# Modulation weight of an adaLN decoder block: products on TensorE in four column tiles in place of VectorE sums, x loaded first

## What is computed

```python
ada = silu(c) @ w_ada + b_ada            # (1024) @ (1024, 6144): one row of 6144
shift1, scale1, gate1, shift2, scale2, gate2 = split(ada, 6)
u = rms_norm(x) * g1 * (1 + scale1) + shift1
proj = u @ w_in                          # S5 input, q, k, v, indexer, two gates
h = x + gate1 * (mixed @ w_out)          # mixed: S5 branch and top-k attention, gated
u2 = rms_norm(h) * g2 * (1 + scale2) + shift2
out = rms_norm(h + gate2 * moe(u2)) * gf # 64 experts, 8 per token
```

## Time and profile before

| | us |
|---|---|
| median of 3 runs (1354.59 to 1357.18) | 1357.01 |
| the profiled execution | 1351.99 |
| its span | 1350.2 |
| TensorE busy | 1191.1 (88%) |
| weight loads (PEld) | 585.5 (43%) |
| VectorE busy | 576.9 (43%) |
| ScalarE busy | 231.8 (17%) |
| GpSimd busy | 266.1 (20%) |
| of VectorE: the 24 sums L1052 | 59.8 |

### The profile page before, as it was taken

The page is one execution under the profiler, slowest core; times in us unless marked ns, Lnnn a source line. Parts: engine busy times, 40 slices in busy tenths (PEclk is TensorE's granted clock), DMA queues, the critical chain, the costliest instruction groups (busy, mean ns, idle before and its releaser), DMA issues. The chain is left out here.

```text
span 1350.2 us, 12868 instructions
## 1 busy us (share of the span) xinstructions
PE 1191.1 (88%) x4460; PEld 585.5 (43%) x4461; DVE 576.9 (43%) x1201; ACT 231.8 (17%) x458; POOL 266.1 (20%) x254
## 2 busy tenths in 40 slices
PE   0799677788999999989789999999999999999954
PEld 0544455444555444435344444444444444444421
DVE  5336899797642403424722222222222222222238
ACT  3412221132334000120011111111111111111111
POOL 7861478100000000020111111111111111111100
PEclk9799787898899999989889999999999999999978
DMA  8635000430404123022789999999999999999276
GB/s 330 172 110 194 9 10 9 164 153 3 187 1 156 63 93 109 32 71 117 295 346 390 371 398 399 400 371 382 398 393 367 378 396 393 360 359 388 82 307 272
DMA packets 85765, 318.35 MB, mean 236 GB/s; under 512 B 30706, under 2 KB 33778, under 8 KB 57026
## 3 DMA queue, kind: packets, MB, share of 16 engines
q1 hardware_dynamic: 64084, 277.96, 53.2%
q0 software_dynamic: 15216, 36.24, 7.1%
q10 hardware_dynamic: 6400, 3.33, 1.1%
HBM read 303.71 MB, written 31.46 MB: 248 GB/s over the span
## 5 line engine op out<-in xcount | busy, mean ns | idle before, releaser
L1506 PE MATMUL ps<-uTs,ring 128*128 128x512 f32 (+2 forms) x496 | 228.2, 618 | 3.7 <-DMA ring<-in_w_in 3.0
L1774 PE MATMUL ps<-ring,XT 128*128 128x512 f32 x512 | 225.1, 592 | 0.4 <-ACT XT L981 0.4
L1368 DVE TENSOR_TENSOR uTs<-uTs,ps 128x256 f32<-128x256 f32 x50 | 21.1, 421 | 300.2 <-ACT uTs L985 300.2
L1506 PEld LDWEIGHTS ps<-uTs,ring 128*128 128x128 f32 (+2 forms) x496 | 95.5, 196 | 123.1 <-issue 118.2
L1774 PEld LDWEIGHTS ps<-ring,XT 128*128 128x128 f32 x512 | 95.1, 191 | 107.7 <-issue 107.1
L721 POOL DMA_INDIRECT XT<-u_rows,idx x51 | 52.0, 1020 | 433.7 <-DVE idx L1357 424.6
L1802 PE MATMUL ps<-ring,XT 128*64 128x512 f32 x576 | 127.6, 595 | 0.9 <-ACT XT L981 0.9
L1813 PE MATMUL ps<-ring,uTs 128*128 128x512 f32 x256 | 119.4, 610 | 0.1
L1409 DVE TENSOR_SCALAR uTs<-ps,gat 128x512 f32<-128x512 f32 x50 | 37.5, 751 | 125.4 <-PE ps L1813 78.9
L1486 PEld LDWEIGHTS ps<-ident,XT 128*128 128x128 f32 x448 | 55.9, 188 | 57.4 <-DMA XT<-u_rows,idx 43.0
L1486 PE MATMUL ps<-ident,XT 128*128 128x128 f32 x448 | 63.8, 287 | 18.5 <-DMA XT<-u_rows,idx 12.4
(11 more groups left out here) (320 smaller groups left out, 1381.0 us busy)
## 6 DMA issues: line engine op xcount, KB each, us to landing
ring<-in_w_exp_gate SPq DMA_DIRECT2D x64, 1024.0 KB, 7.8
ring<-in_w_exp_up SPq DMA_DIRECT2D x64, 1024.0 KB, 12.5
ring<-in_w_exp_down SPq DMA_DIRECT2D x64, 1024.0 KB, 11.5
ring<-in_w_ada SPq DMA_DIRECT2D x12, 2048.0 KB, 12.2
ring<-in_w_in SPq DMA_DIRECT2D x7, 2048.0 KB, 9.4
ring<-expert_rows SPq DMA_DIRECT2D x6, 2048.0 KB, 18.6
ring<-in_w_out SPq DMA_DIRECT2D x2, 2048.0 KB, 8.8
H<-in_x SPq DMA_DIRECT2D x1, 2048.0 KB, 14.2
```

Source lines behind the costliest of these rows:

```text
L1506: ins = mm(b[0:rows_, 0:cols], l, r, start=(k == 0), stop=(k == len(chunks) - 1))
L1774: ins = mm(a3(ps[0][:, :], 2), xgT[par][:, k], wgu[r][:, k], start=(k == 0), stop=(k == KD - 1))
```

## The change

The 24 sums go. A piece is now eight TensorE products into a bank of its own, ps[5]: the stationary side is a column of csil, read 32 times (128x32), the moving side 512 columns of the piece; each of the four 512-column quarters q writes partitions 32q to 32q + 31 of the bank, that is, one of four column tiles. Part by part, `ada_row(part)` adds the bank to the bias, which is loaded ahead 32 times per quarter into 128x512 of ADA; that makes a row per part, `ada_rows[part]`. NB falls from 6 to 5.

The pieces move to TensorE's list: 0 and 1 before the turning of x, 2 and 3 after it, 4 before `indexer(1)`, 5 and 6 in `s5_apply(0)` and `s5_apply(1)` after the transposes of uc, 7 after the four qT products, 8 to 11 after the second, fourth, sixth and eighth gate product of the attention. On VectorE `ada_row(0)` stands after the RMS root, `ada_row(1)` between `top_k(1, 10, 16)` and `top_k(2, 0, 16)`, `ada_row(2)` after the four y2 products. Group mod is four transposes; `ada(n)` picks a row with a column of the identity in place of the ones. The S5 input's first tile waits for the scaled chunks one at a time. SyncE issues x ahead of A0, and the bias of part 0 after A1, of parts 1 and 2 after the S5 tables.

```diff
-NB = 6
+NB = 5
...
+        ada_rows = [ADA[:, 2048:2560], ADA[:, 4096:4608], ADA[:, 4608:5120]]
...
             sp.dma_start(c_in, a["c"][0].rearrange("(p k) -> p k", k=KD)).then_inc(S["c_in"], 16)
 
+            sp.dma_start(H[:], a["x"][0].rearrange("(t p) d -> p t d", p=P)).then_inc(S["x_in"], 16)
+
+            def bias_of_part(part):
+                for q in range(4):
+                    c0 = 2048 * part + 512 * q
+                    sp.dma_start(ada_rows[part][32 * q:32 * (q + 1), :], a["b_ada"][0:1, c0:c0 + 512].broadcast_to((32, 512)))\
+                        .then_inc(b_in[part], 16)
+
             load(("A", 0))
-            sp.dma_start(H[:], a["x"][0].rearrange("(t p) d -> p t d", p=P)).then_inc(S["x_in"], 16)
             load(("A", 1))
-            for n, c in enumerate((slice(0, 2 * DM), slice(2 * DM, 6 * DM))):
-                sp.wait_ge(S["ada_zero"], n + 1)
-                sp.dma_start(ADA[0:1, c], a["b_ada"][0:1, c]).then_inc(b_in[n], 16)
+            bias_of_part(0)
             for g in list(ITEMS)[2:]:
                 if g == ("misc", 0):
                     state_tables()
+                    bias_of_part(1)
+                    bias_of_part(2)
...
-            V.memset(ADA[:, 0:2 * DM], 0.0).then_inc(S["ada_zero"], 1)
-            V.memset(ADA[:, 2 * DM:6 * DM], 0.0).then_inc(S["ada_zero"], 1)
...
-            def ada_piece(n):
-                link(ada_half(n, 0))
-                signal(ada_half(n, 1), "ada_sum", n + 1)
+            def ada_row(part):
+
+                dve.wait_ge(b_in[part], 64)
+                dve.wait_ge(S["ada_sum"], 4 * (part + 1))
+                V.tensor_tensor(ada_rows[part], ada_rows[part], ps[5][:, :], ALU.add).then_inc(S["ada_row"], 1)
...
-            for n in range(2):
-                ada_piece(n)
             dve.wait_ge(S["squares"], 1)
             rms_scale(slice(0, TT), 1)
             V.tensor_copy(junk1, rstd[:, 0:1]).then_inc(S["rstd_ok"], 1)
-            for n in range(2, 4):
-                ada_piece(n)
+            ada_row(0)
...
             s5_kernel(2)
-            ada_piece(6)
             s5_scan(2)
...
             top_k(1, 10, 16)
-            ada_piece(7)
+            ada_row(1)
             top_k(2, 0, 16)
...
-                    if (i, h - 2) in FILL:
-                        k = list(FILL).index((i, h - 2))
-                        if k % 2 == 0:
-                            link(ada_half(8 + k // 2, 0))
-                        else:
-                            signal(ada_half(8 + k // 2, 1), "ada_sum", 9 + k // 2)
...
+            ada_row(2)
             for n in range(4, 12):
+                if n == 9:
+                    done(dve, ("ada", 11))
                 ada_out(n)
...
+            def ada_piece(n):
+
+                part, j = n // 4, n % 4
+                w = a3(arrived(pe, ("A", n)), 2)
+                if n == 0:
+                    pe.wait_ge(S["c_silu"], 1)
+                elif j == 0:
+                    pe.wait_ge(S["ada_row"], part)
+                for k in range(2):
+                    col = csil[:, 2 * j + k:2 * j + k + 1].broadcast_to((P, 32))
+                    for q in range(4):
+                        ins = mm(ps[5][32 * q:32 * (q + 1), :], col, w[:, k, 512 * q:512 * (q + 1)],
+                                 start=(j == 0 and k == 0), stop=(j == 3 and k == 1))
+                ins.then_inc(S["ada_sum"], 1)
+
             def ada(n):
-                pe.wait_ge(S["ada_sum"], 4 * (n // 4 + 1))
-                end(product(("ada", n), [(ones[:], ADA[:, 512 * n:512 * (n + 1)])]))
+                pe.wait_ge(S["ada_row"], n // 4 + 1)
+                row = ident[:, 32 * (n % 4):32 * (n % 4) + 1].broadcast_to((P, P))
+                end(product(("ada", n), [(row, ada_rows[n // 4])]))
...
                 end(ins)
+                if q < 2:
+                    ada_piece(5 + q)
                 taken(pe, ("bT", q, 1))
...
+            ada_piece(0)
+            ada_piece(1)
             for t in range(TT):
                 pe.wait_ge(S["u_tile"], t + 1)
                 transposed_rows("uT", t, ut4)
-            pe.wait_ge(S["ada_sum"], 4)
+            ada_piece(2)
+            ada_piece(3)
+            pe.wait_ge(S["ada_row"], 1)
...
+            ada_piece(4)
             indexer(1)
...
             for m in range(4):
                 projection_t("qT", m, w, P * m)
+            ada_piece(7)
             taken(pe, ("y", NQ - 1, 1))
...
                         projection_t(name, d, a3(arrived(pe, (name, d // 4)), 8), P * (d % 4))
+                        if list(FILL).index((i, h)) % 2:
+                            ada_piece(8 + list(FILL).index((i, h)) // 2)
```

More of the change, by code:

```diff
@@ L260, in build @@
         S = {}
-        for n in """x_in c_in b_in norm_in lam_in ct_in bt_in dt_in dsk_in bglu_in bias_in consts ada_zero
-                c_silu dt_exp angles sines squares u_tile ada_sum pool_turn u_perm inverse root empties ov_em b_ok ba_ok ca_ok w2_ok phase_args phases zeros place_ok sums_ok sums_taken scan_zero g1_in rstd_ok modulation u_ok_v u_ok_s gates_ok toeplitz
+        for n in """x_in c_in b_in norm_in lam_in ct_in bt_in dt_in dsk_in bglu_in bias_in consts
+                c_silu dt_exp angles sines squares u_tile ada_sum ada_row pool_turn u_perm inverse root empties ov_em b_ok ba_ok ca_ok w2_ok phase_args phases zeros place_ok sums_ok sums_taken scan_zero g1_in rstd_ok modulation u_ok_v u_ok_s gates_ok toeplitz
                 u_rows u_chunks rotated relu_free causal dist t_max prob av_done y_att y2_ok mixed h_out
@@ L272, in build @@
         gathered = [ctx.enter_context(nc.semaphore(f"gathered{n}")) for n in range(2)]
-        b_in = [ctx.enter_context(nc.semaphore(f"b_in{n}")) for n in range(2)]
+        b_in = [ctx.enter_context(nc.semaphore(f"b_in{n}")) for n in range(3)]
         rows_in = [ctx.enter_context(nc.semaphore(f"rows_in{n}")) for n in range(2 * TT)]
@@ L1076, in _ @@
             V.tensor_copy(junk1, rstd[:, 0:1]).then_inc(S["rstd_ok"], 1)
-            for n in range(2, 4):
-                ada_piece(n)
+            ada_row(0)
             dve.wait_ge(S["g1_in"], 16)
             b = done(dve, ("mod", 0))
-            V.tensor_copy(shT, b[:, 0:KD])
-            out(V.scalar_tensor_tensor(scT, b[:, KD:2 * KD], 1.0, g1T, ALU.add, ALU.mult), ("mod", 0))
+            b4 = b[:, :].rearrange("p (c q r) -> p q r c", c=4, q=4)[:, :, 0]
+            V.tensor_copy(a3(shT, 2), b4[:, 0:2])
+            out(V.scalar_tensor_tensor(a3(scT, 2), b4[:, 2:4], 1.0, a3(g1T, 2), ALU.add, ALU.mult), ("mod", 0))
             V.tensor_copy(junk1, scT[:, 0:1]).then_inc(S["modulation"], 1)
@@ L1152, in _ @@
                 takes(V.tensor_scalar(Z[:, P * j:P * (j + 1)], b[:, P:2 * P], nsg, None, ALU.mult), ("cT", j))
-            dve.wait_ge(b_in[1], 16)
             dve.wait_ge(S["scan_zero"], 1)
-            ada_piece(4)
             taken(dve, ("vw", 0))
@@ L1159, in _ @@
             s5_phases(0)
-            ada_piece(5)
             index_scores(1)
@@ L1589, in _ @@
                 transposed_rows("uT", t, ut4)
-            pe.wait_ge(S["ada_sum"], 4)
+            ada_piece(2)
+            ada_piece(3)
+            pe.wait_ge(S["ada_row"], 1)
             b = begin(("mod", 0))
-            for c in range(2 * KD):
-                ins = mm(b[:, c:c + 1], ADA[:, P * c:P * (c + 1)], ones[:, 0:1], start=True, stop=True)
+            for c in range(4):
+                ins = tr(b[:, P * c:P * (c + 1)], ada_rows[0][:, P * c:P * (c + 1)])
             end(ins)
-            pe.wait_ge(S["u_ok_v"], KD // 2)
-            pe.wait_ge(S["u_ok_s"], KD // 2)
             w = a3(arrived(pe, ("ssm", 0)), 8)
             for t in range(TT):
-                end(product(("ssm", t), [(uT[:, k, P * t:P * (t + 1)], w[:, k]) for k in range(KD)]))
+                b = begin(("ssm", t))
+                for k in range(KD):
+                    if t == 0:
+                        pe.wait_ge(S["u_ok_s" if k % 2 else "u_ok_v"], k // 2 + 1)
+                    ins = mm(b[:, :], uT[:, k, P * t:P * (t + 1)], w[:, k], start=(k == 0), stop=(k == KD - 1))
+                end(ins)
             pe.wait_ge(S["ct_in"], 256)
```

## The result

The changed kernel takes 1363.97 us (median of 20 runs, 1354.64 to 1369.01) against 1356.09 us (20 runs of the kernel before beside it, 1352.72 to 1359.47): ratio 1.0048, 95% interval 1.0033 to 1.0062. It is slower by half a per cent. The profiled execution took 1366.27 us, span 1364.5, mean granted clock 0.944 (before: 1351.99, 1350.2, 0.949).

A forecast was written before the change was run, and what follows sets the result against it. It took the chain of waits before the expert weights, roughly the first 450 us, as the bound. Terms -16.7 + 1.7 - 4.0 + 17.5 + 6.9 + 1.0 = +6.4 us on the median 1357.01 gave 1363.4 us, range 1354 to 1381.

The forecast's parts named there:

- (a): Start: first input-weight product at 37 us instead of 52.09, plus half of 3.3 us of lower clock won; -16.7 us.
- GpSimd's condition: At the start, ScalarE's scaling waits for GpSimd's angles: ready at 30 us instead of 40.7, else ScalarE 8 us late.
- (b): Piece 4 goes onto TensorE ahead of the indexer, whose products everything waits for: +1.7 us.
- (c): Pieces 5 and 6 cost nothing in TensorE's waits after the uc transposes; VectorE loses 5.32 us of sums: -4 us.
- (d): Before the attention, ada_row(1) waits for piece 7 after q, holding back top_k(2), 20.0 us: +17.5 us.
- (e): Pieces 8 to 11 in the attention add four times 1.7 us to TensorE: +6.9 us, 0 if hidden.
- (f): ada_row(2) after the four y2 products starts part 2's broadcast 1 us later: +1.0 us; five banks 0, up to 2.
- the last rival: VectorE and GpSimd come apart between 126 and 262 us, up to 9 us extra gain: 1353.9 us, chance 0.13.
- three times instead of four: Four column tiles bring only a factor of three, 2.3 us a piece: 1367.6 us, chance 0.12.
- two tiles: Four column tiles gain no more than two, 3.4 us a piece: 1379.2 us, chance 0.15.
- serial at 6.9: A piece's products run one after another, 6.9 us a piece: about 1414 us, chance 0.03.
- The start gained less: Angles stay late or first products at the lower clock, start gains 8 instead of 16.7 us: 1372.1 us, chance 0.09.

The follow-up runs named there:

- run 8: Kernel of run 1 with pieces 8, 9 and 10 moved behind the first two score products of attention blocks 1, 2 and 3: 1335.92 us, ratio 0.9826.
- run 1: Changed kernel with ada_row(1) moved behind top_k(2) instead of ahead of it: 1349.52 us, ratio 0.9944 to the kernel before.
- run 2: Changed kernel with x loaded behind A0 again, as before the change: 1364.5 us, ratio 1.006 to the kernel before.
- run 5: Changed kernel with the second half of pieces 8 to 11 left out: 1359.65 us, ratio 1.0024 to the kernel before.
- run 6: Changed kernel with a piece's two loops exchanged, both products of a column tile following each other: 1363.65 us, ratio 1.0048 to the kernel before.
- run 7: Changed kernel with three unused VectorE sums of 128x1536 put where piece 6 was: 1366.64 us, ratio 1.007 to the kernel before.
- run 9: Changed kernel with pieces 8, 9 and 10 moved as in run 8, ada_row(1) staying ahead of top_k(2): 1352.42 us, ratio 0.9974 to the kernel before.
- run 4: Kernel before with five banks instead of six, nothing else: 1355.35 us, ratio 0.9998.
- run 3: Kernel before with only the load order changed, x ahead of A0 and the first bias row between A0 and A1: 1352.82 us, ratio 0.9969.
- run 10: Kernel before with five banks and 16 unneeded products behind the first two score products of blocks 1 to 3: 1349.69 us, ratio 0.9951.

## Why the prediction was right, and where it was not

It said 1363.4 us and the median is 1363.97, and the mechanism, a gain at the start eaten up by the wait of ada_row(1), is the one the runs show. So near a hit is partly luck: it was a difference of 6.4 us on a median of 1357.01, and the measured one is 7.9 on a median of 1356.09. The steps tell more.

(a) Start: -14.0 measured, -16.7 said. The first product came at 38.1 instead of 37: the last slice landed 1.7 us later than worked out (32.3 against 30.6), and the rest of the chain was 0.6 shorter. The other 1.6 us were the half of the lower clock that I counted as won. In this profile it was not: from 38.12 to the transposes at 68.39 the stage took 30.3 us, before 30.5. The windows of the changed kernel (columns as in run 8) show the clock still down as the stage begins:

```profile
32.00:36.00 4.00, 2.80 (x17) 0.55 (x18) 0.69 (x1) 0.00 (x0) 3.21 (x11) 0.67 1.05 388
36.00:40.00 4.00, 2.86 (x7) 1.46 (x8) 2.21 (x7) 2.45 (x4) 3.70 (x5) 0.50 0.88 122
40.00:44.00 4.00, 4.00 (x7) 1.70 (x6) 0.00 (x0) 0.48 (x1) 3.63 (x5) 0.55 0.68 70
44.00:54.00 10.00, 10.00 (x25) 4.49 (x24) 0.00 (x0) 0.60 (x1) 9.45 (x8) 1.00 0.46 102
```

TensorE had been busier, but with waits of 3.12, 0.87 and 1.14 us between. The half was a guess with no row behind it, and one profile doesn't settle it: the stage took 29.3 us in runs 1, 2, 5, 6 and 7 (which start it at 38.5 to 39.4), 30.2 and 30.6 in runs 8 and 9, and with the old start 30.5, 30.6, 30.4 and 29.1 (before, runs 4, 3 and 10). The clock moves it by over 1 us from execution to execution. GpSimd's condition held: the operation that took 3.09 us beside a sum takes 0.93, also while TensorE reads the weight. That agrees with the port rule of the Trainium skill ("SBUF — State Buffer") named in the prediction. The angles are ready at 27.95 instead of 30, because the prediction priced eight operations at 0.93 us; seven lay beside sums (17.0 us together), and alone those take 0.43 to 0.93, 5.1 together.

(b) Piece 4: 1.85 us from its start to the indexer's, 1.7 said.

(c) VectorE without piece 6: -3.5 in the profile, -3.9 by the mean of all profiles (138.2 us with the sums, 134.3 without), -4 said. The size is right, but the reason is not shown: 7.7 us of sums put back in run 7 gave back about 1 us. In this profile TensorE waits 5.36 us for GpSimd at 216.23, which it does in runs 5 and 8 too, but not in 1, 2, 6 and 9, and the stretch is as long in either.

(d) The wait of ada_row(1): from q to gate product 0 before 38.2 us, after 55.7. +17.5, the number said. In run 1's profile it is 38.2 again, all of it taken back; its runs show 14 us. The steps inside are as worked out too: 20.0 us of top_k(2) from 279.33, and gate product 0 5.4 us behind it.

(e) Pieces 8 to 11: +9.1 between gate product 0 and the broadcasts, +6.9 said. A piece is 1.86 us to the next start (325.76 to 327.61), so four are 7.4. TensorE is idle for 7.9 us of the stretch in both profiles, so nothing of the pieces was hidden, and the remaining 1.7 are busy time. I put them down to the lower clock, which fell otherwise on the gate products (counted from 0, number 4 took 9.03 us against 8.08, number 6 8.70 against 7.03, number 2 8.21 against 8.60). The other profiles bear that out: the stretch takes 142.1 to 145.8 us in the five with the changed attention (after, runs 1, 2, 6 and 7; mean 144.5) and 136.5 to 137.9 in the three with the old one (before, runs 3 and 4; mean 137.0). The means are 7.5 us apart, the pieces and no more. What the prediction missed altogether is that the waits at the block starts were there to be filled, and that filling them is worth about twice the pieces (12.2 us in the profiles of runs 8 and 9 for three pieces of 1.86, or 8.6 against the shortest of those five stretches).

(f) ada_row(2): +1.0 as said, of which the wait for VectorE is 0.46. Five banks: 0 (run 4).

The steps as measured make +11.7 at the output projection, not +6.4, and the profiles' +14.3 at the end has 2.6 more, 1.5 of it busy time of TensorE; why is not shown. The medians are only 7.9 apart: the profiled run of before lies 4.1 below its median, that of after 2.3 above, which is the difference. By the two profiles (a) gained 2.7 us less and (e) cost 2.2 more than said; against the medians the sum is 1.5 short. With means over all profiles that have a stretch in the same form, the terms are (a) -14.2 (counted to the end of the first stage), (b) +1.9, (c) -3.9, (d) +16.4, (e) +7.5 and (f) +0.9, together +8.6. (d) is smaller there because the q projection alone, 27.7 us in most, took 29.4 and 30.7 in the profiles of runs 3 and 10.

Two workings on record don't hold. The forecast's own bounds, added as independent, come to some 1356 to 1373 us and not 1357 to 1369. And the 13.25 us against 3.61 of the last rival compare sums over 384 and over 256 columns; at equal width the ratio is 2.4, not 3.7.

The rivals: three times instead of four, 2.3 us a piece, and two tiles, 3.4 us, are excluded by 1.86 us, and so is serial at 6.9. The measured piece is 3.7 times faster than full width. Against the estimate of 2.2 us from the Trainium skill ("TensorE: Matmul & The Clock Gate", packing small matmuls), the trace decides: four column tiles gain more here than its factors for three column tiles and for four row tiles. The start gained less than said, but by 2.7 and not 8.7. VectorE and GpSimd did not come apart: the same seven sums take 13.27 us at 123.41.

## What to carry to other kernels

Moving work to an idle engine moves its consumer's wait as well: look for what is queued behind that wait on the receiving engine (here 20 us of sorting, which cost more than the whole start gained), and put the consumer behind it. Small products that must go somewhere belong in TensorE's short waits: in runs 8 and 9 they took the place of idle time, and the granted clock behind them stayed up. A term taken from the clock's lower level needs a row that shows the level change, and more than one profile: the same code lay up to 3.7 us apart here.

## What the hardware showed that was not expected

- Four column tiles of 32, float32, 128x32 by 128x512: 16 records in 1.86 us start to start, against 6.9 for the 16 of full width; the order of issue makes no difference (1.0048 both).
- 48 useless records made the kernel before 0.47% faster than the same kernel without them (0.9951 against 0.9998), with the granted clock at 1.00 from 325 to 440 us in place of 0.85 and 0.96.
- Piece 0 took 3.64 us (15.64) and piece 1 1.92 (21.06), where the windows of 12 to 24 us read a granted clock of 1.00; in run 6 both took 3.67, and in runs 1, 7 and 8 piece 1 took 3.56 to 3.64. What halves the pace there is not in the granted clock. The cause stays open.
- The runs of one kernel lie 14 us apart, and the clock goes with it: five of the changed kernel's 20 have a mean granted clock of at most 0.944 and take 1363.39 to 1369.01 us; the four with 0.951 or more take 1354.64 to 1359.53. A single profile of each kernel would have said 1.1% where 20 runs say 0.5%.
